# w_ada summed slot by slot on VectorE, and w_in and w_conv_out slots of 512 columns by 512 rows

## The reference

```python
mod = jnp.einsum('bd,dm->bm', silu(c), w_ada) + b_ada          # 1024 x 6144, one row of c
shift_m, scale_m, gate_m, shift_f, scale_f, gate_f = jnp.split(mod, 6, axis=-1)
h = modulate(rms_norm(x, g_norm_mix), shift_m, scale_m)
p = jnp.einsum('bsd,dk->bsk', h, w_in)                         # 1024 x 5632
u_f, v, b_g, c_g, g_logits = split of p                        # 512, 1024, 1024, 1024, 2048 columns
y_a = fourier_mix(u_f) @ w_fourier
y_b = (b_g * centred_conv3(c_g * v, w_conv)) @ w_conv_out
z = sigmoid(g_logits a) * y_a + sigmoid(g_logits b) * y_b
x = x + gate_m * (z @ w_o)
...  # router, 16 experts of 1024 x 2048 x 3 matrices, then the second block
```

## Time and profile before

| | |
|---|---|
| time, median of 3 runs | 1363.65 us (1363.28 to 1365.02) |
| time of the profiled execution | 1364.12 us |
| its span, first to last instruction | 1362.3 us |
| TensorE busy | 1008.5 us (74%) |
| VectorE busy | 338.4 us (25%) |
| ScalarE busy | 239.4 us (18%) |
| moved by DMA | 496.38 MB, mean 364 GB/s |

### The profile page before, as it was taken

How to read it: one execution, slowest core, us unless ns; L and a number is a source line. 1 busy time by engine, 2 the same in 40 slices (tenths; PEclk the granted TensorE clock), 3 DMA queues, 4 the chain that set the end, 5 groups by cost and what they waited for, 6 DMA issues and landing times.

```text
span 1362.3 us, 15741 instructions
## 1 busy us (share of the span) xinstructions
PE 1008.5 (74%) x6817; PEld 522.3 (38%) x6817; DVE 338.4 (25%) x490; ACT 239.4 (18%) x350; POOL 25.1 (2%) x81
## 2 busy tenths in 40 slices
PE   5999999796766666575665656666665666799998
PEld 1889989521211111111111111111111111399988
DVE  2556347510000000000000000000000000378875
ACT  2423434200000000000000000000000000366655
POOL 1000010000000000000000000000000000000000
PEclk8899999798978688887878877788788878999999
DMA  9997796799999999999999999999999999984330
GB/s 369 380 327 252 253 299 239 327 390 430 425 429 429 427 429 429 427 429 429 428 429 429 428 428 430 428 428 430 428 428 430 427 428 429 347 278 140 110 124 32
DMA packets 89609, 496.38 MB, mean 364 GB/s; under 512 B 5160, under 2 KB 57804, under 8 KB 61148
## 3 DMA queue, kind: packets, MB, share of 16 engines
q1 hardware_dynamic: 87616, 489.31, 88.6%
q0 software_dynamic: 1568, 6.24, 1.3%
q10 hardware_dynamic: 380, 0.16, 0.0%
HBM read 494.64 MB, written 1.05 MB: 364 GB/s over the span
## 4 chain that ended last, share of the span: by engine, by line
DMA 61%; PE 35%; DVE 2%; issue 1%; ACT 1%; SPq 0%; ACTq 0%
DMA ring<-in_w_up_e 21%; DMA ring<-in_w_down_e 19%; DMA ring<-in_w_gate_e 19%; PE psum L608 8%; PE psum L610 8%; PE psum L609 8%; PE psum L903 4%; PE psum L929 2%; PE psum L674 1%; DMA ring<-in_w_ada 1%; DMA ring<-in_w_in 1%; PE psum L965 1%; PE psum L729 1%; DVE ring_r L1437 0%; PE psum L666 0%
## 5 line engine op out<-in xcount | busy, mean ns | idle before, releaser
L903 PE MATMUL psum<-ring,arena 128*32 128x512 f32 x2048 | 305.6, 728 | 199.3 <-DMA ring<-in_w_up_e 116.8
L929 PE MATMUL psum<-ring,arena 128*32 128x512 f32 x992 | 171.5, 807 | 91.8 <-DMA ring<-in_w_down_e 84.3
L903 PEld LDWEIGHTS psum<-ring,arena 128*32 128x32 f32 x2048 | 61.1, 122 | 399.8 <-DMA ring<-in_w_up_e 157.0
L1437 DVE TENSOR_TENSOR ring_r<-ring,ring_r 128x2048 fp32r<-128x2048 f32 x55 | 124.6, 2288 | 65.0 <-ACT ring_r L1116 64.8
L608 PE MATMUL psum<-ring_r,ht_hi 128*128 128x256 f32 (+1 forms) x384 | 114.5, 298 | 5.5 <-DVE ht_lo L1441 5.2
L929 PEld LDWEIGHTS psum<-ring,arena 128*32 128x32 f32 x992 | 35.8, 130 | 209.8 <-DMA ring<-in_w_down_e 146.2
L1116 ACT ACTIVATE ring_r<-ring 128x2048 fp32r<-128x2048 f32 x55 | 103.9, 1910 | 57.9 <-PE psum L610 32.9
L610 PE MATMUL psum<-ring_r,ht_lo 128*128 128x256 f32 (+1 forms) x384 | 113.3, 295 | 0.0
L609 PE MATMUL psum<-ring_r,ht_hi 128*128 128x256 f32 (+1 forms) x384 | 112.9, 294 | 0.0
L608 PE MATMUL psum<-ht_hi,ring_r 128*128 128x256 f32 x384 | 108.3, 282 | 0.0
L610 PE MATMUL psum<-ht_hi,ring_r 128*128 128x256 f32 x384 | 107.2, 279 | 0.0
(11 more groups left out here) (258 smaller groups left out, 753.2 us busy)
## 6 DMA issues: line engine op xcount, KB each, us to landing
ring<-in_w_gate_e SPq DMA_DIRECT2D x64, 2048.0 KB, 36.4
ring<-in_w_up_e SPq DMA_DIRECT2D x64, 2048.0 KB, 35.8
ring<-in_w_down_e SPq DMA_DIRECT2D x58, 2048.0 KB, 35.9
ring<-in_w_in SPq DMA_DIRECT2D x38, 1024.0 KB, 10.1
ring<-in_w_ada SPq DMA_DIRECT2D x24, 1024.0 KB, 11.1
ring<-in_w_down_e SPq DMA_DIRECT2D x8, 1024.0 KB, 22.5
ring<-in_w_conv_out SPq DMA_DIRECT2D x4, 1024.0 KB, 5.5
ring<-in_w_o SPq DMA_DIRECT2D x4, 1024.0 KB, 13.1
```

The costliest lines, as they stand in the source:

```text
L903: last = mm(psum[32 * g:32 * g + 32, b, :], cur[h][:, k, :], w[:, g, :], start=(k == 0), stop=(k == KD - 1), tile_position=(0, 32 * g))
L929: last = mm(psum[32 * q:32 * q + 32, 2 + n, :], act_t[:, f % 4, (f // 4) * CAP:(f // 4 + 1) * CAP], w[:, kk, n * BANK:(n + 1) * BANK], sta ...
L1437: V.tensor_tensor(ring_r[place(s)][:], ring[:, place(s), :], ring_r[part_place[s]][:].bitcast(F32), ALU.subtract).then_inc(lo_ready, 1)
```

## The change

- **w_ada on VectorE.** For each of ada1 and ada2 ScalarE multiplies the first slot by its silu(c) column in place (`weigh_ada`); VectorE makes slot k = slot k * c[k] + slot k − 1 for k = 1 to 7 (`add_ada`); TensorE then sums the last slot over the partitions with four products of ones (`sum_partitions`) ahead of units ga1 and yb0. A slot of w_ada may be loaded over only when the next add has read it (`sum_moved_on`, waited for on SyncE).
- **Placement.** `ADA_PER_UNIT` spreads the 16 slots over units 1, 2, 6, 7, 8, 10 to 16. VectorE's add for the slots ahead of unit u + 1 is issued in unit u, behind the splits and ahead of that unit's evictions.
- **Slots of 512 by 512.** w_in and w_conv_out come as two halves of the rows with all 512 columns (`row_halves`, pieces of 2 KB). `half_products` does the upper rows for both banks, then the lower rows for both banks; the first bank is complete after three quarters of the unit. fourier_in's matmuls have 512 columns (`first_product`), 48 instead of 96.

```diff
-ADA_BEFORE = {u: [divmod(n, KD)] for n, u in enumerate(list(range(1, 13)))}
-ADA_BEFORE |= {14: [divmod(12, KD), divmod(13, KD)], 15: [divmod(14, KD)], 16: [divmod(15, KD)]}
-ADA_BEFORE = {u: [(1 + b, k) for b, k in steps] for u, steps in ADA_BEFORE.items()}
+ADA_PER_UNIT = {1: 1, 2: 1, 6: 1, 7: 1, 8: 1, 10: 1, 11: 2, 12: 2, 13: 1, 14: 1, 15: 2, 16: 2}
+ADA_ORDER = iter([(b, k) for b in (1, 2) for k in range(KD)])
+ADA_BEFORE = {u: [next(ADA_ORDER) for _ in range(n)] for u, n in ADA_PER_UNIT.items()}
...
+        def row_halves(w, chunk):
+            return [rows_of(w, (chunk * BANK, (chunk + 1) * BANK), FG * i, FG) for i in range(2)]
...
+        def sum_moved_on(eng, s):
+            if s in ada_slot:
+                b, k = ada_slot[s]
+                if k == KD - 1:
+                    eng.wait_ge(ada_summed, b)
+                else:
+                    eng.wait_ge(ada_added, ada_adds_before[b, k + 1])
...
                 if s >= HEAD_RING:
                     sp.wait_ge(slot_used, s - HEAD_RING + 1)
+                    sum_moved_on(sp, s - HEAD_RING)
...
+            def half_products(s, u, act_parts, others=0):
+                for i in range(2):
+                    w = split_slot(s + i, k=FG, n=BANK)
+                    for j in range(2):
+                        for c in range(2):
+                            at = slice((2 * j + c) * P, (2 * j + c + 1) * P)
+                            for kk in range(FG):
+                                k = FG * i + kk
+                                last = split_product(bank(2 * (u % 2) + j, c=2, s=SEQ)[:, c, :], [h[:, kk, at] for h in w],
+                                                     [a[:, k, :] for a in act_parts], k == 0 and c == 0, k == KD - 1 and c == 1)
+                        if i and j == 0:
+                            end_first(last)
+                    last.then_inc(slot_used, 1 if i else 1 + others)
...
+            def first_product(s, u, await_k):
+                for i in range(2):
+                    w = split_slot(s + i, k=FG, n=BANK)
+                    for tt in range(TT):
+                        for kk in range(FG):
+                            k = FG * i + kk
+                            if tt == 0:
+                                await_k(k)
+                            last = split_product(bank(2 * (u % 2) + tt), [a[:, k, tt * P:(tt + 1) * P] for a in (ht_hi, ht_lo)],
+                                                 [h[:, kk, :] for h in w], k == 0, k == KD - 1)
...
+            def sum_partitions(b, to):
+                pe.wait_ge(ada_added, ada_adds_before[b, KD - 1])
+                for g in range(4):
+                    last = mm(psum[32 * g:32 * g + 32, to, :], ones[:, 0:32], slot_in(first_slot[f"ada{b}_{KD - 1}"], g=4, n=512)[:, g, :],
+                              start=True, stop=True, tile_position=(0, 32 * g))
+                last.then_inc(ada_summed, 1)
...
             for u, (name, slots) in enumerate(HEAD_UNITS):
-                for bk in ADA_BEFORE.get(u, ()):
-                    if bk == (1, 0):
-                        pe.wait_ge(mod_ready, 1)
-                    modulation(*bk, 3 + bk[0])
+                for b, k in ADA_BEFORE.get(u, ()):
+                    if k == KD - 1:
+                        if b == 1:
+                            pe.wait_ge(mod_ready, 1)
+                        sum_partitions(b, 3 + b)
...
+            def weigh_ada(b, k):                     # ScalarE
+                s = first_slot[f"ada{b}_{k}"]
+                arrived(act, s)
+                w = ring[:, place(s), :]
+                f(w, w, ACT.Copy, scale=c_act[:, k:k + 1]).then_inc(ada_weighted, 1)
...
+            def add_ada(b, k):                       # VectorE
+                s = first_slot[f"ada{b}_{k}"]
+                arrived(dve, s)
+                w, before = (ring[:, place(first_slot[f"ada{b}_{n}"]), :] for n in (k, k - 1))
+                if k == 1:
+                    dve.wait_ge(ada_weighted, b)
+                else:
+                    dve.wait_ge(ada_added, ada_adds_before[b, k - 1])
+                V.scalar_tensor_tensor(w, w, c_act[:, k:k + 1], before, ALU.mult, ALU.add).then_inc(ada_added, 1)
...
             for u, (name, _) in enumerate(HEAD_UNITS):
                 b = 2 * (u % 2)
                 split_ahead(head_ahead[u])
+                for part, k in ADA_BEFORE.get(u + 1, ()):
+                    if k:
+                        add_ada(part, k)
```

More of the change, by code:

```diff
@@ L273, in build @@
         gate_row_done, gate_row_ready = sem("gate_row_done"), sem("gate_row_ready")
+        ada_weighted, ada_added, ada_summed = sem("ada_slots_weighted"), sem("ada_slots_added"), sem("ada_partitions_summed")
         squared, mean_ready, root_ready, scale_ready, xr_ready = (sem(n) for n in ("squared", "mean_ready", "root_ready", "scale_ready", "xr_ready"))
@@ L323, in build @@
             if name in IN_CHUNK:
-                head_stream += columns(w_in, 2, 2 * IN_CHUNK[name])
+                head_stream += row_halves(w_in, IN_CHUNK[name])
             elif name in ("ya0", "ya1"):
@@ L328, in build @@
             elif name in ("yb0", "yb1"):
-                head_stream += columns(t["w_conv_out"][0], 2, 2 * int(name[2]))
+                head_stream += row_halves(t["w_conv_out"][0], int(name[2]))
         first_slot["w_o"] = len(head_stream)
@@ L412, in plan @@
             for u, (name, slots) in enumerate(units):
-                if slots == 2 and name not in ROWS_UNITS:
+                if slots == 2 and name not in ROWS_UNITS and tag == "tail":
                     ready_at[tag, u, 0] = (slot_used, first_slot[name] + 1)
@@ L445, in gate_bank, with ada_before @@
             return (4 + c if c < 2 else c - 2) + 2 * tt
+        ada_steps = [bk for u in sorted(ADA_BEFORE) for bk in ADA_BEFORE[u]]
+        ada_adds_before = {(b, k): (KD - 1) * (b - 1) + k for b, k in ada_steps}
+        ada_slot = {first_slot[f"ada{b}_{k}"]: (b, k) for b, k in ada_steps}
+        def ada_before(u):
+            since = max((v for v in range(u) if HEAD_UNITS[v][1]), default=-1)
+            return sum(len(ADA_BEFORE.get(v, ())) for v in range(since + 1, u + 1))
+        def sum_moved_on(eng, s):
[5 more added lines that the diff above has]
+                    eng.wait_ge(ada_added, ada_adds_before[b, k + 1])
         head_u = {name: u for u, (name, _) in enumerate(HEAD_UNITS)}
@@ L498, in _ @@
                 sp.wait_ge(slot_used, HEAD_SLOTS - HEAD_RING + 2 * d + 2)
+                for s in range(HEAD_SLOTS - HEAD_RING + 2 * d, HEAD_SLOTS - HEAD_RING + 2 * d + 2):
+                    sum_moved_on(sp, s)
                 load_first(d)
@@ L628, in transposed_product @@
                     last.then_inc(slot_used, 1)
+            def half_products(s, u, act_parts, others=0):
[21 more added lines that the diff above has]
+                                                 [h[:, kk, :] for h in w], k == 0, k == KD - 1)
+                        if i and tt == 0:
+                            end_first(last)
+                    last.then_inc(slot_used, 1)
             def columns_rows(s, to, act_parts, await_k=None, before_last=None):
@@ L667, in turn_norm, with modulation @@
                     last.then_inc(norm_turned, 1)
-            def modulation(b, k, to):
-                s = first_slot[f"ada{b}_{k}"]
+            def sum_partitions(b, to):
[4 more added lines that the diff above has]
+                last.then_inc(ada_summed, 1)
+            def modulation(k, to):
+                s = first_slot[f"ada0_{k}"]
                 arrived(pe, s)
@@ L719, in _ @@
                 if name in IN_CHUNK:
-                    transposed_product(first_slot[name], u, (ht_hi, ht_lo))
+                    half_products(first_slot[name], u, (ht_hi, ht_lo), ada_before(u))
                 elif name in ("seq01", "seq23"):
@@ L748, in _ @@
                                                      (fm_hi[:, k, :], fm_lo[:, k, :]), k == 0, k == FG - 1)
-                        end_first(last) if j == 0 else end_second(last, slots)
+                        end_first(last) if j == 0 else end_second(last, slots + ada_before(u))
                 else:
                     pe.wait_ge(st_ready, 4)
-                    transposed_product(first_slot[name], u, (st_hi, st_lo))
+                    half_products(first_slot[name], u, (st_hi, st_lo), ada_before(u))
                     if name == "yb0":
@@ L1130, in _ @@
             roots(0)
+            def weigh_ada(b, k):
[3 more added lines that the diff above has]
+                f(w, w, ACT.Copy, scale=c_act[:, k:k + 1]).then_inc(ada_weighted, 1)
             def modulation_rows(b, from_bank):
-                act.wait_ge(slot_used, first_slot[f"ada{b}_{KD - 1}"] + 1)
+                if b:
+                    act.wait_ge(ada_summed, b)
+                else:
+                    act.wait_ge(slot_used, first_slot[f"ada0_{KD - 1}"] + 1)
```

(8 more changed lines are left out.)

6 lines of the change are left out of this document (3 added, 3 removed).

## The result

The changed kernel takes 1354.56 us (median of 4 runs, 1353.76 to 1356.77) against 1363.53 (1363.28 to 1365.02): a ratio of 0.9938, interval 0.9924 to 0.9952. It is faster by 9.0 us. 1350.0 was forecast, 13.6 less.

What follows compares the result with a forecast made beforehand. The head was taken as bound by TensorE's instruction stream, with the end moving one for one with the first expert's start. 17.6 + 0.9 − 2.4 − 2.5 = 13.6 us less than 1363.65: 1350.0, range 1346 to 1355.

Steps and rivals of the forecast that it cites:

- the lateness of transfers: Head, SyncE's slot loads: held w_ada slots delay later loads, but each is 4 us or more ahead; cost nothing.
- the second wait: TensorE after gb1, ahead of yb0: waits 0.4 us for VectorE's last two adds before ada2's sum.
- What is removed: TensorE in the head: 16 steps of w_ada, four fp32 products each, go; 17.6 us less.
- fourier_in: Start of the head: six matmuls of 512 columns do more work inside TensorE's wait for the norm; 0.9 us gained.
- the two sums: Added on TensorE ahead of ga1 and yb0: two sums over partitions, 1.19 us each, 2.4 us.
- that case: Rival without new waits in the head: adds find room or VectorE runs ahead; 16.1 us less, 1347.5; chance 0.12.
- The price of an add: VectorE in the head: each of 14 scalar_tensor_tensor of 128x2048 takes 2.2 us, 31 us in all.
- The rival "slower": VectorE's adds in the head take 4.4 us each, waits of 21.5; 5.4 us slower, 1369; chance 0.05.
- The first wait: TensorE after ga0, ahead of ga1: waits 2.1 us for VectorE's adds (1,6) and (1,7) before the sum.
- it has just caught up: VectorE from ga1 to yb0: gb0's first half is split 0.6 us before TensorE wants it.
- signs of being wrong: Adds over 3 us, TensorE waiting for w_in or w_fourier, half clock in the head, DMA not idle before first expert.
- The rival "more waits than I count": Head: clock falls to half around the 2.1 us wait, or a slot is late; 5 to 11 less; chance 0.2.

Runs made afterwards that it cites:

- every new wait taken out: The changed kernel with both sums over partitions moved from ahead of ga1 and yb0 to the middle of these units: 1346.61 us, ratio 0.9877.
- the run with both edits: The changed kernel with the sums in the middle of ga1 and yb0 and GpSimd's side loads behind gb1: 1347.5 us, ratio 0.9877.
- the adds alone: w_ada on VectorE as in the change, but slots of 256 columns in 1 KB pieces as before: 1356.15 us, ratio 0.9952 against the kernel before.

## Why the prediction was off

The sign, the place and the mechanism of the gain were right. One term of the costs was wrong: the lateness of transfers, put at nothing. It made the second wait 4.2 us longer than forecast, and 1.4 us of half clock followed.

- **What is removed (17.6), fourier_in (0.9), the two sums (2.4).** With every new wait taken out, the first expert comes 16.3 us earlier (15.7 in the run with both edits); the prediction's sum for that case is 16.1. fourier_in is worth 0.8 by the adds alone against the change, 1.2 by the change against before; TensorE's wait there is 4.0 instead of 5.2. v0's second matmul is at 49.54 (49.7 forecast). From v0 on the gain is 15.0 and 14.8 us, predicted 15.2; that each single step cost what I gave it isn't shown.
- **A misreading without effect.** The granted clock is not 1.00 in every window from 40 us on: from 40 to 60 us it is 0.93.
- **The price of an add.** Predicted 2.2 us, measured 2.35 for each of 14. The rule of the Trainium skill, "Vector Engine (DVE) Microarchitecture Reference", section 7, that such an instruction with two SBUF sources that are not bf16 halves throughput would have given an estimate of 4.4, twice the 2.2; the trace disagrees, since a tensor_tensor of that size takes 2.29 us. The rival "slower" went with it.
- **The first wait.** Predicted 2.1, measured 2.21, with no fall of the clock in the change's profile. That the clock stayed up was in part luck: of five profiled executions with this wait one, that with only the b_ada rows moved, had a fall behind it that cost 1.4 us.
- **VectorE between ga1 and yb0.** "it has just caught up" was right: gb0's last eviction is at 177.57 (177.6 forecast). The experiment with an add moved ahead shows how small the cover was: of the add's 2.3 us TensorE waited 2.06.
- **Transfers, the step that failed.** "The later slots I followed in the same way: each is 4 us or more ahead of its use. Cost nothing". The slot is the second of w_conv_out, issued at 170.24. With the 5.3 us of a lone slot it would have landed at 175.5, 4.7 us before ScalarE was free for it at 180.2: that is the cover the prediction claims. It landed at 184.37. The prediction takes one rate for the whole head and nowhere names what GpSimd's queue loads. The trace of before had the warning: 132 and 174 GB/s in the windows above, at the same place of the program. It cost nothing there, because the slots of w_conv_out were issued ahead of the side loads and those that ran beside them weren't wanted yet. With the adds the second slot waits for VectorE and is under way while the side loads are. That the side loads are what delays it is shown by moving them (5.5 us instead of 14.1); that an issue 5 us earlier isn't enough, by the add moved ahead (15.2 us). How they delay it stays open. Among its signs of being wrong the prediction had TensorE waiting for a slot of w_in or w_fourier, but not of w_conv_out.
- **The second wait.** Predicted 0.4; 4.56 measured, and 1.4 of half clock behind it: 4.2 + 1.4 = 5.6 us, against the 13.6 − 8.07 = 5.5 us that the first expert fell short. With the side loads moved the wait is 0.7, and the time 1350.02 where 1350.0 was forecast.
- **The rival "more waits than I count"** named both parts, a late slot and a fall of the clock, with 5 to 11 less than before; 9.0 it is. It had a chance of 0.2. The ground for costing transfers at nothing was that nothing in the head had waited for a slot. That says nothing of a kernel in which the slots are issued by another rule.
- **From the first expert on** the span moved one for one with it, to within the spread of 2 us between executions.

## What to carry to other kernels

When a change makes a load wait for another engine, place the load at its new time in the trace and read the bandwidth of that stretch, with every queue that loads there, in windows of a few microseconds; a mean over the head hides a hole of 4 us. Where a short product can stand anywhere in a unit, put it where its sources have been ready for long, not at the boundary: that was worth 8 us here and made the late slot harmless. And when work is moved to an engine that was half idle, follow that engine's order up to the next thing that it makes for the bottleneck; an add of 2.3 us put ahead of the next unit's split made TensorE wait 2.1 us there and then run 3.3 us at half clock.

## What the runs showed of the hardware

- 1.25 MB of small and broadcast loads on GpSimd's queue lengthened the landing of a 1 MB slot on SyncE's from 5.5 to 14.1 us, and the core's rate fell to 101 GB/s over 4 us. The same loads 23 us later left the rate at 351 GB/s and more.
- The same wait of TensorE of 2.21 us, at the same place of the program and ahead of the same eight short records, was followed by 2.8 us at half clock in one profiled execution and by none in four others. Waits of 2.06, 2.69 and 4.56 us were each followed by about 3 us at half clock. Neither the length of the wait nor the instructions around it alone tell whether the clock falls.
- scalar_tensor_tensor of 128x2048 fp32 takes 2.35 us, within 3% of tensor_tensor.
